# Five pieces of index work moved under the expert loop, and half of the combine's rows gathered before the last expert's are stored

## The chip, the cores and the metric

One NeuronCore of one Trainium2 chip runs the kernel. The metric is the device time of one execution in microseconds. Its engines are TensorE (PE in the profile; PEld is its weight load), VectorE (DVE), ScalarE (ACT), GpSimd (POOL) and SyncE (SP), which only issues transfers here.

## The reference

Two transformer blocks run one after the other on 512 tokens of width 1024, in float32. What the change touches is the end of the second block, a mixture of experts:

```python
g_sel = argmax(g_logits)                     # one group of 4 experts for each token
top_val, top_idx = lax.top_k(e_sel_logits, 2)   # two experts of that group
top_w = softmax(top_val) * g_w
hid = silu(xs @ w_gate[e]) * (xs @ w_up[e])  # 1024 -> 512, for each chosen e
x = x + sum over the two e of top_w * (hid @ w_down[e])   # 512 -> 1024
```

Each token goes to two of 16 experts, so 1024 rows of expert results exist in all, and every token adds two of them, weighted.

## The kernel before, in words

**Everything up to about 1831 us** (the first block, attention and recurrence of the second, the router) is untouched by the change.

**The router** leaves in the tile R (SBUF, one row of small arrays per partition, four tokens to a partition) the choices (R_M), the weights (R_W) and each token's place within its experts (R_P). `rows_of` holds, expert by expert, the 128 tokens that it takes first.

**The expert loop.** Expert e takes up to 128 tokens. GpSimd gathers their rows of `h_rows` from DRAM with an indirect transfer (L2659). PE transposes them (L1182), multiplies by gate and up (`into_hidden`, L1200), transposes the hidden row (`turn_hidden`, L1215) and multiplies by down (`out_of_hidden`, L1220). All products are made in three passes, from an upper and a lower part of each operand, so every weight granule (2 MB) has to be split before use: ACT writes the upper part in two halves (`weights_up`, L1784, instruction L1800), DVE the lower part in two halves (`weights_low`, L2380, instruction L2384). PE waits for each half by `w_low_made`. Raw weights lie in 4 slots, upper halves in 6.

**The order of the work** in the loop is written out by hand on each engine, and each engine runs its own list in order. PE (L1291): gate of e+1, transposes of the hidden row of e, up of e+1, transposes of the tokens of e+2, down of e. DVE (L2412 to L2423): the two lower halves of up e+1, the lower part of hidden row e (`hidden_low`, L2403), the two halves of down e, the product of gate and up of e+1 (`expert_hidden`, L2397), the lower part of the tokens of e+2 (`expert_low`, L2391), and then the two halves of gate e+2. ACT (L1838 to L1851): the two upper halves of up, the Silu of e+1 (L1814), the upper part of hidden row e (L1820), the copy of the result of e-1 out of PSUM (L1826) and its store to `y_rows` in DRAM (L1829), the two upper halves of down e, the tokens' upper part (L1807), the two halves of gate e+2. PE's gate of e+2 starts when its first lower half is made.

**The index work of the combine** stands on DVE behind the loop, L2426 to L2475: 37 small operations, most with a wait on the one before (`chain`). It has two results. `over` (L2447) says how many further tiles of 128 tokens are needed where an expert was chosen by more than 128 tokens; all engines read that count and run a loop of that many trips. `back_rows` (L2475) holds for each token the two rows of `y_rows` that are its results: in columns 0 to 3 the higher row of each of the four tokens, in 4 to 7 the lower.

**The combine.** ACT signals `all_stored` (L1868) once all 16 stores have landed (`y_main`) and further tiles, if any, have too. GpSimd waits for `back_rows` and for `all_stored`, and issues eight gathers of 128 rows of 4 KB (512 KB each, L2676), two for each block of 128 tokens. DVE waits for both rows of a block, adds them to `x_tok` in two operations (L2506), and SP stores the block (L692).

Of the kernel before, what the change touches and what calls it, by code (L numbers as in the profile page):

```python
# [18 lines left out]
U32 = mybir.dt.uint32  # L19
# [173 lines left out]
def program(nc, a, out, known=None, debug=None):  # L193
    n = Counts(known)
    mark, at, now = n.mark, n.at, n.now
    with ExitStack() as ctx:
# [9 lines left out]
        def sem(name):  # L206
            return ctx.enter_context(nc.semaphore(name))
# [29 lines left out]
        back_rows = sb("back_rows", [P, 8], U32)  # L237
        over_i = sb("over_i", [P, 1 + OVER], I32)
# [129 lines left out]
        rows_back = [sem(f"rows_back{i}") for i in range(QT)]  # L368

# [1502 lines left out]
        def _(dve):  # L1872
# [531 lines left out]

            for j in range(4):
                weights_low(j)
# [5 lines left out]
            for e in range(EXPERTS - 1):  # L2412
                j = 2 * granule_no["gate", e + 1]
                weights_low(j + 2)
                weights_low(j + 3)
                hidden_low(e)
                weights_low(j + 4)
                weights_low(j + 5)
                expert_hidden(e + 1)
                if e + 2 < EXPERTS:  # L2420
                    expert_low(e + 2)
                weights_low(j + 6)
                weights_low(j + 7)  # L2423
            hidden_low(EXPERTS - 1)

            chain(stt(out=R[:, R_Q:R_Q + 64], in0=R[:, R_P:R_P + 64], scalar=1.0, in1=R[:, R_M:R_M + 64],  # L2426
                      op0=ALU.add, op1=ALU.mult))
            chain(ts(R[:, R_Q:R_Q + 64], R[:, R_Q:R_Q + 64], -1.0, None, ALU.add))
            places = r(R_Q, QT, 16)

            counts = R[:, R_P + 64:R_P + 80].unsqueeze(1).to_broadcast([P, 3, 16])
            edges = const[:, K_OT:K_OT + 48].rearrange("p (t e) -> p t e", t=3)
            chain(tt(r(R_A, 3, 16), counts, edges, ALU.is_gt))
            flags = R[:, R_A:R_A + 48]
            chain(nc.vector.tensor_tensor_scan(R[:, R_A + 48:R_A + 96], const[:, K_ONES:K_ONES + 48], flags, 0.0,
                                               ALU.mult, ALU.add))
            shape = [P, OVER, 48]
            lst, lst2 = r(R_V, OVER, 48), r(R_V + OVER * 48, OVER, 48)
            chain(tt(lst, R[:, R_A + 48:R_A + 96].unsqueeze(1).to_broadcast(shape),
                     spread(const[:, K_NTH:K_NTH + OVER], 48), ALU.is_equal))  # L2440
            chain(tt(lst, lst, flags.unsqueeze(1).to_broadcast(shape), ALU.mult))
            chain(tt(lst2, lst, const[:, K_OT:K_OT + 48].unsqueeze(1).to_broadcast(shape), ALU.mult))
            chain(nc.vector.tensor_reduce(over_t[:, :], lst2, AX.X, ALU.add))
            chain(tt(lst, lst, const[:, K_OE:K_OE + 48].unsqueeze(1).to_broadcast(shape), ALU.mult))
            chain(nc.vector.tensor_reduce(R[:, R_B + 1:R_B + 1 + OVER], lst, AX.X, ALU.add))
            chain(nc.vector.tensor_copy(R[:, R_B:R_B + 1], R[:, R_A + 95:R_A + 96]))
            made(nc.vector.tensor_copy(over_i[:, :], R[:, R_B:R_B + 1 + OVER]), "over")  # L2447


            first = const[:, K_FIRST:K_FIRST + 16].unsqueeze(1).to_broadcast([P, QT, 16])  # L2450
            chain(tt(r(R_V, QT, 16), r(R_P, QT, 16), first, ALU.add))

            base = R[:, R_A + 48:R_A + 96]
            step = R[:, R_A + 96:R_A + 144]
            chain(ts(base, base, float(P), float((EXPERTS - 1) * P + 1), ALU.mult, ALU.add))
            chain(tt(base, base, const[:, K_OT:K_OT + 48], ALU.subtract))
            chain(tt(step[:, 16:48], base[:, 16:48], base[:, 0:32], ALU.subtract))
            chain(tt(step[:, 0:16], base[:, 0:16], const[:, K_FIRST:K_FIRST + 16], ALU.subtract))
            for t in range(3):
                beyond = r(R_A + 144, QT, 16)  # L2460
                chain(ts(beyond, r(R_P, QT, 16), float(P * (t + 1)), None, ALU.is_ge))
                chain(tt(beyond, beyond, step[:, 16 * t:16 * t + 16].unsqueeze(1).to_broadcast([P, QT, 16]),
                         ALU.mult))
                chain(tt(r(R_V, QT, 16), r(R_V, QT, 16), beyond, ALU.add))
            chain(tt(R[:, R_V:R_V + 64], R[:, R_V:R_V + 64], R[:, R_M:R_M + 64], ALU.mult))
            chain(nc.vector.tensor_reduce(R[:, R_S:R_S + 4], r(R_V, QT, 16), AX.X, ALU.max))
            chain(nc.vector.tensor_reduce(R[:, R_S + 4:R_S + 8], r(R_V, QT, 16), AX.X, ALU.add))
            chain(tt(r(R_A, QT, 16), r(R_V, QT, 16), spread(R[:, R_S:R_S + 4], 16), ALU.is_equal))
            chain(tt(R[:, R_A:R_A + 64], R[:, R_A:R_A + 64], R[:, R_W:R_W + 64], ALU.mult))
            chain(nc.vector.tensor_reduce(R[:, R_WT:R_WT + 4], r(R_A, QT, 16), AX.X, ALU.add))  # L2470
            chain(tt(R[:, R_A:R_A + 64], R[:, R_W:R_W + 64], R[:, R_A:R_A + 64], ALU.subtract))
            chain(nc.vector.tensor_reduce(R[:, R_WT + 4:R_WT + 8], r(R_A, QT, 16), AX.X, ALU.add))
            chain(tt(R[:, R_S + 4:R_S + 8], R[:, R_S + 4:R_S + 8], R[:, R_S:R_S + 4], ALU.subtract))
            chain(ts(R[:, R_S:R_S + 8], R[:, R_S:R_S + 8], -1.0, None, ALU.add))
            made(nc.vector.tensor_copy(back_rows[:, :], R[:, R_S:R_S + 8]), "back_rows")  # L2475
# [26 lines left out]

            for i in range(QT):
                dve.wait_ge(rows_back[i], 32)
                for j in range(2):
                    ins = stt(out=x_tok[:, i, :], in0=returned[:, 2 * i + j, :],  # L2506
                              scalar=R[:, R_WT + 4 * j + i:R_WT + 4 * j + i + 1], in1=x_tok[:, i, :],
                              op0=ALU.mult, op1=ALU.add)
                    if j == 0:

                        ins.then_inc(summed, 1)
                        dve.wait_ge(summed, i + 1)
                ins.then_inc(combined, 1)
# [3 lines left out]
        def _(pool):  # L2517
# [195 lines left out]
```

## Time and profile before

| | |
|---|---|
| three runs | 2173.44 us median (2172.85 to 2177.55) |
| the profiled execution | 2180.36 us |
| its span | 2178.3 us |
| busy: PE, DVE, ACT, POOL | 91%, 59%, 41%, 16% of the span |
| expert loop, about 1831 to 2150 us | per expert some 19.3 us |

The span is what the profiler saw of the engines' work; the execution's own time lies 2.06 us above it. All durations in the text come from the profiled execution.

### The profile page before, as it was taken

Reading aid. Unit: us, or ns where it says so; the run is one execution under the profiler, and the core shown is the slowest. Engines: PE = TensorE matmul, PEld = TensorE weight load, DVE = VectorE, ACT = ScalarE, POOL = GpSimd, SP = SyncE. Lnnn points to the kernel's source line nnn. Section 1 sums busy time; section 2 is a strip of 40 time slices with the busy share of each in tenths; the row PEclk is TensorE's granted clock in tenths of the full one; section 3 lists DMA queues with packets and bytes.
Section 4 is the critical chain, followed back from the end, with each engine's and each line's share of the span. In section 5 each row is a group of like instructions: output and inputs, shape, how many; then the busy total and the mean of one; then the engine's idle time right before and its main releaser. Section 6 shows DMA issues by size and latency. Waiting matters only on the chain.

```text
span 2178.3 us, 27413 instructions
## 1 busy us (share of the span) xinstructions
PE 1983.1 (91%) x11088; PEld 1593.3 (73%) x11088; DVE 1276.1 (59%) x1587; ACT 898.3 (41%) x1476; POOL 351.7 (16%) x259
## 2 busy tenths in 40 slices
PE   5999899999899989999989897888999997999994
PEld 4965678899796667889967695666556876777773
DVE  5449744344444974434448927666665335788886
ACT  3323333333232334333333325543764323777772
POOL 4120122100412012210041104550000001000001
PEclk9999889999799989999989999999999996999997
DMA  4202110223220111022212220012124233999994
GB/s 141 79 24 63 39 40 20 78 80 96 66 78 25 50 52 40 22 76 90 95 64 73 77 68 30 20 40 77 60 76 164 97 135 115 373 386 383 381 373 189
DMA packets 159873, 241.58 MB, mean 111 GB/s; under 512 B 8754, under 2 KB 106195, under 8 KB 159747
## 3 DMA queue, kind: packets, MB, share of 16 engines
q1 hardware_dynamic: 152370, 213.01, 29.0%
q0 software_dynamic: 4464, 16.25, 2.0%
q10 hardware_dynamic: 2912, 10.55, 1.2%
q8 instruction: 90, 1.47, 0.3%
q14 instruction: 37, 0.30, 0.0%
HBM read 223.55 MB, written 16.25 MB: 110 GB/s over the span
## 4 chain that ended last, share of the span: by engine, by line
PE 73%; DVE 20%; issue 2%; ACT 2%; DMA 1%; POOL 0%; ACTq 0%; POOLq 0%; DVEq 0%
PE acc L756 28%; PE acc L983 15%; PE acc L1196 8%; DVE work L1943 5%; PE acc L968 4%; PE acc L735 3%; PE acc L913 3%; PE acc L1048 2%; PE acc L890 2%; DVE ring_split L2384 2%; DVE v L2128 1%; PE acc L1106 1%; DVE rt L2198 1%; PE acc L901 1%; DVE ring L1959 1%
## 5 line engine op out<-in xcount | busy, mean ns | idle before, releaser
L756 PE MATMUL acc<-h_split,ring_split 128*128 128x264 f32 x1088 | 312.9, 288 | 0.0
L756 PE MATMUL acc<-h_split,v_split 128*128 128x264 f32 (+1 forms) x736 | 212.5, 289 | 9.8 <-DVE ring_split L1948 8.5
L756 PE MATMUL acc<-ring_split,v_split 128*128 128x264 f32 (+1 forms) x736 | 209.8, 285 | 0.0
L756 PEld LDWEIGHTS acc<-h_split,ring_split 128*128 128x128 f32 x1088 | 209.4, 192 | 0.0
L1948 DVE TENSOR_TENSOR ring_split<-ring,v_split 128x1024 fp32r<-128x1024 f32 (+1 forms) x78 | 92.3, 1185 | 177.6 <-ACT v_split L1355 177.6
L756 PEld LDWEIGHTS acc<-h_split,v_split 128*128 128x128 f32 (+1 forms) x736 | 138.9, 189 | 13.3 <-issue 9.8
L983 PE MATMUL acc<-h_split,ring_split 128*128 128x512 f32 x368 | 145.4, 395 | 0.0
L1943 DVE RECIPROCAL work<-work 96x528 f32<-96x528 f32 (+1 forms) x38 | 130.9, 3445 | 24.2 <-ACT work L1385 23.8
L756 PEld LDWEIGHTS acc<-ring_split,v_split 128*128 128x128 f32 (+1 forms) x736 | 139.0, 189 | 0.1
L735 PE MATMUL acc<-latent,ring 128*96 128x264 f32 (+1 forms) x512 | 119.9, 390 | 0.0
L1355 ACT ACTIVATE v_split<-ring 128x1024 fp32r<-128x1024 f32 x80 | 77.5, 971 | 84.6 <-PE acc L756 80.0
L756 PE MATMUL acc<-h_split,krope_split 128*128 128x264 f32 x320 | 95.6, 299 | 16.2 <-DVE work L2017 13.2
L735 PEld LDWEIGHTS acc<-latent,ring 128*96 128x96 f32 (+1 forms) x512 | 77.5, 156 | 42.8 <-issue 9.4
L2128 DVE RECIPROCAL v<-v 128x512 f32<-128x512 f32 x26 | 87.1, 3351 | 24.7 <-ACT v L1564 24.7
L2067 DVE TENSOR_TENSOR acc<-acc,const 128x128 f32<-128x128 f32 (+1 forms) x80 | 21.7, 272 | 132.5 <-PE acc L890 132.2
L756 PE MATMUL acc<-ring_split,krope_split 128*128 128x264 f32 x320 | 92.2, 288 | 0.0
L2551 POOL TENSOR_TENSOR ring_split<-ring,krope_split 128x1024 fp32r<-128x1024 f32 x20 | 47.3, 2363 | 265.1 <-ACT krope_split L1355 265.1
L2538 POOL TENSOR_TENSOR latent<-latent 128x528 f32<-128x528 f32 x21 | 32.0, 1525 | 322.3 <-ACT latent L1350 321.8
L1196 PE MATMUL acc<-qk_split,krope_split 128*128 128x512 f32 x240 | 75.8, 397 | 8.6 <-DVE ring_split L2384 6.2
L2659 POOL DMA_INDIRECT latent<-h_rows,rows_of x16 | 18.3, 1145 | 396.7 <-PE acc L1182 229.4
L983 PEld LDWEIGHTS acc<-h_split,ring_split 128*128 128x128 f32 x368 | 69.7, 189 | 16.2
L913 PE MATMUL acc<-latent,v 128*64 128x128 f32 (+2 forms) x480 | 79.1, 289 | 0.0
(485 smaller groups left out, 5407.6 us busy)
## 6 DMA issues: line engine op xcount, KB each, us to landing
ring<-in_w_in SPq DMA_DIRECT2D x64, 1024.0 KB, 5.2
ring<-in_w_expert_gate SPq DMA_DIRECT2D x13, 2048.0 KB, 10.4
ring<-in_w_expert_up SPq DMA_DIRECT2D x12, 2048.0 KB, 11.3
ring<-in_w_expert_down SPq DMA_DIRECT2D x11, 2048.0 KB, 11.7
ring<-in_w_out SPq DMA_DIRECT2D x12, 1024.0 KB, 5.3
hres<-in_w_expert_down SPq DMA_DIRECT2D x5, 2048.0 KB, 11.2
hres<-in_w_expert_up SPq DMA_DIRECT2D x4, 2048.0 KB, 11.2
y_rows<-gate ACTq DMA_DIRECT2D x16, 512.0 KB, 7.1
```

Of the source, the lines that this page charges most:

```text
L735: ins = nc.tensor.matmul(dst[at_row:at_row + rows_, half, 0:HALF], w, rhs(k)[:, half * HALF:(half + 1) * HALF], start=(k == 0), stop=(k == ...
L756: ins = nc.tensor.matmul(dst[0:rows_, half, 0:HALF], w[:, k, :], x[:, c], start=(k == 0 and i == 0), stop=(k == last and i == 2), skip_gro ...
L890: ins = nc.tensor.matmul(dst[0:nt, c0:c1], qT[0:QK, hd, t0:t0 + nt], kT[0:QK, hd, c0:c1], start=True, stop=True)
L913: ins = nc.tensor.matmul(dst[r:r + VD, 0, 0:nt], v[0:nk, j, hd * VD:(hd + 1) * VD], probsT[s % 2][0:nk, j, 0:nt], start=(j == 0), stop=(j ...
L968: ins = nc.tensor.matmul(dst[:, 0, :], w, rhs(k), start=(k == 0), stop=(k == len(lhs) - 1))
L983: ins = nc.tensor.matmul(dst[:, 0, :], w[:, k, :], x, start=(k == 0 and i == 0), stop=(k == DC - 1 and i == 2), skip_group_check=True)
L1196: ins = nc.tensor.matmul(dst, x, w, start=start and i == 0, stop=stop and i == 2, skip_group_check=True)
L1355: nc.scalar.activation(dst, src, ACT.Copy).then_inc(act_made, 1)
L1943: chain(nc.vector.reciprocal(work[0:rows_, tile, :], work[0:rows_, tile, :]))
L1948: made(nc.vector.tensor_tensor(dst, src, up.bitcast(F32), ALU.subtract), label)
L2128: chain(nc.vector.reciprocal(tmp[tile], tmp[tile]))
L2551: nc.gpsimd.tensor_tensor(dst, src, up.bitcast(F32), ALU.subtract).then_inc(pool_made, 1)
```

## The change

The 37 operations are the same but for two more, and are cut into five functions. They are called on DVE in the trips e = 3, 5, 7, 9 and 11 of the expert loop, between `expert_low(e + 2)` and the two lower halves of gate e+2. The last of them makes a second list, `early_rows`: the lower row of each token, limited to the rows of the first 15 experts. GpSimd gathers these four lists once the results of the first 15 experts have landed, before it reads `over`. Once all is stored it gathers only the four lists of higher rows. If there are further tiles, it gathers the lower rows again after them. DVE adds the four early rows first, then the four late ones. The early rows go to places 0 to 3 of `returned`, the late ones to places 4 to 7, which overlap the buffers of upper halves.

```diff
@@ DVE, in the expert loop
                 if e + 2 < EXPERTS:
                     expert_low(e + 2)
+                if e == 3:
+                    places_of_rows()
+                elif e == 5:
+                    over_rows()
+                elif e == 7:
+                    main_rows()
+                elif e == 9:
+                    later_rows()
+                elif e == 11:
+                    rows_of_tokens()
                 weights_low(j + 6)
                 weights_low(j + 7)
@@ DVE, the end of rows_of_tokens (the rest of the five is L2426 to L2475 in the same order)
+                chain(ts(R[:, R_S + 8:R_S + 12], R[:, R_S + 4:R_S + 8], float((EXPERTS - 1) * P - 1), None, ALU.min))
+                nc.vector.tensor_copy(early_rows[:, :], R[:, R_S + 8:R_S + 12])
                 made(nc.vector.tensor_copy(back_rows[:, :], R[:, R_S:R_S + 8]), "back_rows")
@@ DVE, the combine (inside "if tiles > 0", behind its loop: wait for rows_early[i] >= 32)
-            for i in range(QT):
-                dve.wait_ge(rows_back[i], 32)
-                for j in range(2):
...
+            for i in range(QT):
+                dve.wait_ge(rows_early[i], 16)
+                add_row(i, i, R_WT + QT + i).then_inc(summed, 1)
+            for i in range(QT):
+                dve.wait_ge(rows_back[i], 16)
+                dve.wait_ge(summed, i + 1)
+                add_row(i, QT + i, R_WT + i).then_inc(combined, 1)
@@ GpSimd
+            pool.wait_ge(dve_made, at(dve_made, "back_rows"))
+            pool.wait_ge(y_main, 16 * (EXPERTS - 1))
+            for i in range(QT):
+                nc.gpsimd.indirect_dma_start(returned[:, i, :], None, y_rows[0:(EXPERTS - 1) * P, :],
+                                             bass.IndirectOffsetOnAxis(early_rows[:, i:i + 1], 0))\
+                    .then_inc(rows_early[i], 16)
             pool.wait_ge(dve_made, at(dve_made, "over"))
             tiles = pool.value_load(over_i[0:1, 0:1], min_val=0, max_val=OVER)
             with pool.If(tiles > 0):
...
+                pool.wait_ge(all_stored, 1)
+                for i in range(QT):
+                    pool.wait_ge(rows_early[i], 16)
+                    nc.gpsimd.indirect_dma_start(returned[:, i, :], None, y_rows,
+                                                 bass.IndirectOffsetOnAxis(back_rows[:, QT + i:QT + i + 1], 0))\
+                        .then_inc(rows_early[i], 16)
-            pool.wait_ge(dve_made, at(dve_made, "back_rows"))
             pool.wait_ge(all_stored, 1)
             for i in range(QT):
-                for j in range(2):
-                    nc.gpsimd.indirect_dma_start(returned[:, 2 * i + j, :], None, y_rows,
-                                                 bass.IndirectOffsetOnAxis(back_rows[:, 4 * j + i:4 * j + i + 1], 0))\
-                        .then_inc(rows_back[i], 16)
+                nc.gpsimd.indirect_dma_start(returned[:, QT + i, :], None, y_rows,
+                                             bass.IndirectOffsetOnAxis(back_rows[:, i:i + 1], 0))\
+                    .then_inc(rows_back[i], 16)
```

## Rows read from the trace of the kernel before

**Rows 1.** The page: its first line, and section 4, the chain by engine.

```profile
span 2178.3 us, 27413 instructions
...
PE 73%; DVE 20%; issue 2%; ACT 2%; DMA 1%; POOL 0%; ACTq 0%; POOLq 0%; DVEq 0%
```

**Rows 2.** Waits of PE, 1880 to 2145: total us, times, longest.

```profile
PE acc L1196 <- DVE ring_split L2384: 10.2, 20, 1.4
PE acc L1196 <- DVE hres_split L2384: 3.6, 7, 0.6
PE acc L1196 <- ACT gate L1826: 1.8, 1, 1.8
```

**Rows 3.** Windows, expert loop; after the busy times: PEclk, DMA share, GB/s.

```profile
1960.00:2145.00 185.00, 173.21 (x793) 138.44 (x792) 152.27 (x91) 133.52 (x96) 6.70 (x7) 1.00 0.95 351
```

**Rows 4.** Chain, 1960 to 2002: start, us, what.

```profile
1969.10 5.81 PE acc L1196 x24
...
1982.08 2.32 DVE ring_split L2384
...
1986.13 2.21 DVE hres_split L2384
...
1988.47 5.70 PE acc L1196 x24
```

**Rows 5.** ACT timeline, 1910 to 1990: start, us, operation, [idle before it <-releaser].

```profile
1975.44 0.60 ACT L1814 ACTIVATE v<-acc 128x512 f32<-128x512 f32 x1 [4.79 <-PE acc L1217]
...
1977.92 3.72 ACT L1800 ACTIVATE qk_split<-ring 128x2048 fp32r<-128x2048 f32 x2 [0.47 <-ACT gate L1826]
```

**Rows 6.** DVE timeline, 1910 to 1990.

```profile
1976.56 0.69 DVE L2403 TENSOR_TENSOR krope_split<-acc,krope_split 128x512 fp32r<-128x512 f32 x1 [1.01 <-ACT krope_split L1820]
1979.87 4.53 DVE L2384 TENSOR_TENSOR ring_split<-ring,qk_split 128x2048 fp32r<-128x2048 f32 x2 [2.62 <-ACT qk_split L1800]
```

**Rows 7.** DVE timeline, 2110 to 2179: first operation of each piece, and the last.

```profile
2144.25 0.22 DVE L2426 SCALAR_TENSOR_TENSOR o<-o 128x64 f32<-128x64 f32 x1
...
2146.35 0.51 DVE L2442 TENSOR_TENSOR o<-o,const 128x336 f32<-128x336 f32 x1
...
2148.78 0.22 DVE L2451 TENSOR_TENSOR o<-o,const 128x64 f32<-128x64 f32 x1
...
2149.93 0.20 DVE L2461 TENSOR_SCALAR o<-o 128x64 f32<-128x64 f32 x1
...
2152.18 0.23 DVE L2465 TENSOR_TENSOR o<-o 128x64 f32<-128x64 f32 x1
...
2154.63 0.17 DVE L2475 CAST back_rows<-o 128x8 uint32<-128x8 f32 x1
```

**Rows 8.** Chain, 2140 to 2179.

```profile
2151.47 2.64 DMA y_rows<-gate
...
2155.95 0.94 POOL qk L2676
```

**Rows 9.** ACT timeline, 2140 to 2179.

```profile
2144.45 0.34 ACTq L1829 DMA_DIRECT2D y_rows<-gate  x1
```

**Rows 10.** Line 2676, the eight gathers: durations, first and last start, landing.

```profile
L2676 POOL DMA_INDIRECT qk<-y_rows,back_rows x8: 936/938/1310, 2156.0 to 2165.0; - x8
...
DMA to landing us min/median/max: 4.1/6.1/7.7
```

**Rows 11.** DVE timeline, 2110 to 2179: sums that waited for rows.

```profile
2166.09 5.12 DVE L2506 SCALAR_TENSOR_TENSOR work<-qk,o,work 128x1024 f32<-128x1024 f32 x4 [0.87 <-DMA qk<-y_rows,back_rows]
2172.72 2.61 DVE L2506 SCALAR_TENSOR_TENSOR work<-qk,o,work 128x1024 f32<-128x1024 f32 x2 [1.50 <-DMA qk<-y_rows,back_rows]
```

**Rows 12.** Line 1829, the sixteen stores of expert results: landing.

```profile
DMA to landing us min/median/max: 2.6/7.1/7.9
```

**Rows 13.** DMA issues, 2165.2 to 2165.6: size, us to landing.

```profile
out<-work SPq DMA_DIRECT2D x1, 512.0 KB, 6.8
```

**Rows 14.** DMA issues, 2168 to 2170.

```profile
out<-work SPq DMA_DIRECT2D x1, 512.0 KB, 4.9
```

More of the change, by code:

```diff
@@ L237, in program @@
         back_rows = sb("back_rows", [P, 8], U32)
+        early_rows = sb("early_rows", [P, QT], U32)
         over_i = sb("over_i", [P, 1 + OVER], I32)
@@ L368, in program @@
         rows_back = [sem(f"rows_back{i}") for i in range(QT)]
+        rows_early = [sem(f"rows_early{i}") for i in range(QT)]
         held = sem("held")
@@ L2403, in hidden_low, with places_of_rows @@
                 evacuated(tt(ht_low, acc[:, 3, 0, :], ht_up.bitcast(F32), ALU.subtract), ("ht", e))
+            places = r(R_Q, QT, 16)
+            shape = [P, OVER, 48]
+            lst, lst2 = r(R_V, OVER, 48), r(R_V + OVER * 48, OVER, 48)
+            flags = R[:, R_A:R_A + 48]
+            base = R[:, R_A + 48:R_A + 96]
+            step = R[:, R_A + 96:R_A + 144]
+            def places_of_rows():
+                chain(stt(out=R[:, R_Q:R_Q + 64], in0=R[:, R_P:R_P + 64], scalar=1.0, in1=R[:, R_M:R_M + 64],
+                          op0=ALU.add, op1=ALU.mult))
+                chain(ts(R[:, R_Q:R_Q + 64], R[:, R_Q:R_Q + 64], -1.0, None, ALU.add))
+                counts = R[:, R_P + 64:R_P + 80].unsqueeze(1).to_broadcast([P, 3, 16])
+                edges = const[:, K_OT:K_OT + 48].rearrange("p (t e) -> p t e", t=3)
+                chain(tt(r(R_A, 3, 16), counts, edges, ALU.is_gt))
+                chain(nc.vector.tensor_tensor_scan(R[:, R_A + 48:R_A + 96], const[:, K_ONES:K_ONES + 48], flags, 0.0,
+                                                   ALU.mult, ALU.add))
+                chain(tt(lst, R[:, R_A + 48:R_A + 96].unsqueeze(1).to_broadcast(shape),
+                         spread(const[:, K_NTH:K_NTH + OVER], 48), ALU.is_equal))
+                chain(tt(lst, lst, flags.unsqueeze(1).to_broadcast(shape), ALU.mult))
@@ new lines, in over_rows @@
+            def over_rows():
+                chain(tt(lst2, lst, const[:, K_OT:K_OT + 48].unsqueeze(1).to_broadcast(shape), ALU.mult))
+                chain(nc.vector.tensor_reduce(over_t[:, :], lst2, AX.X, ALU.add))
+                chain(tt(lst, lst, const[:, K_OE:K_OE + 48].unsqueeze(1).to_broadcast(shape), ALU.mult))
+                chain(nc.vector.tensor_reduce(R[:, R_B + 1:R_B + 1 + OVER], lst, AX.X, ALU.add))
+                chain(nc.vector.tensor_copy(R[:, R_B:R_B + 1], R[:, R_A + 95:R_A + 96]))
+                made(nc.vector.tensor_copy(over_i[:, :], R[:, R_B:R_B + 1 + OVER]), "over")
@@ new lines, in main_rows @@
+            def main_rows():
+                first = const[:, K_FIRST:K_FIRST + 16].unsqueeze(1).to_broadcast([P, QT, 16])
+                chain(tt(r(R_V, QT, 16), r(R_P, QT, 16), first, ALU.add))
+                chain(ts(base, base, float(P), float((EXPERTS - 1) * P + 1), ALU.mult, ALU.add))
+                chain(tt(base, base, const[:, K_OT:K_OT + 48], ALU.subtract))
+                chain(tt(step[:, 16:48], base[:, 16:48], base[:, 0:32], ALU.subtract))
+                chain(tt(step[:, 0:16], base[:, 0:16], const[:, K_FIRST:K_FIRST + 16], ALU.subtract))
@@ L2424, in _ @@
             hidden_low(EXPERTS - 1)
[L2426 to L2447, printed above, removed]
@@ L2450, in _ @@
[L2450 to L2471, printed above, removed]
@@ L2472, in _ @@
[L2472 to L2475, printed above, removed]
             def hidden(tag):
@@ L2501, in _, with add_row @@
                     n.leave()
-            for i in range(QT):
-                dve.wait_ge(rows_back[i], 32)
-                for j in range(2):
[L2506 to L2513, printed above, removed]
+                for i in range(QT):
+                    dve.wait_ge(rows_early[i], 32)
+            def add_row(i, row, weight_):
+                return stt(out=x_tok[:, i, :], in0=returned[:, row, :], scalar=R[:, weight_:weight_ + 1],
+                           in1=x_tok[:, i, :], op0=ALU.mult, op1=ALU.add)
+            for i in range(QT):
+                dve.wait_ge(rows_early[i], 16)
[4 more added lines that the diff above has]
+                add_row(i, QT + i, R_WT + i).then_inc(combined, 1)
         @block.gpsimd
```

19 lines of the change are left out of this document (added).

## The prediction

> **What bounds the kernel now.** I read the page first: PE is 73% of the chain that ended last, DVE 20% [rows 1]. That share is an average, so the next question was who ends PE's waits in the stretch where the new work is put. Over the expert loop PE waits 15.6 us, and 13.8 of them, in 27 waits, end with a lower half made by DVE (L2384) [rows 2]; the TensorE clock there is 1.00, its 2.4 GHz level, and DMA is 95% busy [rows 3].
>
> The chain of waits then shows where in an expert this happens. One period is 19.37 us, from the start of one gate product to the next (1969.10 to 1988.47) [rows 4]. It closes as a ring with no slack in it. The gate product ends at 1974.91 and four transposes follow; ACT has sat idle 4.79 us for them and starts at 1975.44 [rows 5]. It works through Silu, hidden row, result copy and store issue, and begins the upper halves of down at 1977.92. DVE has been idle for the first of these halves for 2.62 us and starts at 1979.87 [rows 6]. From there it never stops: two lower halves, the product (L2397), the tokens' lower part (L2391), and from 1986.13 the first lower half of the next gate, on which PE starts at 1988.47 [rows 4]. The new pieces go between L2391 and that half: on the ring, in front of the instruction that PE waits for.
>
> At the end the order is another. The index work runs from 2144.25 to 2154.80 [rows 7] beside PE's last down product, ACT's last copy and the last store, which is issued at 2151.47 and lands 2.64 us later; after some handing over GpSimd starts its gathers at 2155.95 [rows 8]. back_rows is ready 1.15 us before that. So the index work costs nothing today, and taking it away from there gains nothing. The real gain has to come from what lies behind 2155.95: eight gathers, eight sums, stores, 22.35 us up to the span's end at 2178.3.
>
> **The change, step by step. The five pieces in the loop.** Their costs are differences of starts in the trace of today [rows 7]: 2.10 us (2144.25 to 2146.35), 2.43, 1.15, 2.25, and for the last piece 2.45 to the start of L2475, 0.17 for it, and two new operations of the same small kind, which I price at 0.20 and 0.17 after their neighbours: 2.99. Together 10.92 us. Each piece stands in one period on the ring, so PE's gate starts that much later, ACT's Silu after it as well, and every later period with it. Nothing gives it back: PE already waits in front of that product (0.4 us of its wait is there now), and DVE's two idle stretches, 1.01 and 2.62 us [rows 6], end with ACT operations that themselves follow the delayed gate. The bounds are 10.9 (all exposed) and 0 (all absorbed in those 3.6 us per expert, more than any one piece takes); I take **+10.9**, because the ring accounts for the whole period.
>
> The waits that the pieces add (`chain`) are waits of DVE on itself and are inside the differences. Queued behind them on DVE are the gate halves, which is the cost just counted. ACT, SP and GpSimd get no new wait in the loop. GpSimd's gathers of tokens come once per expert and shift with PE.
>
> **The late gathers.** Now four follow `all_stored` in place of eight. A lone gather lands 4.1 us after its issue, and issues are 1.29 us apart ((2165.0 - 2156.0)/7) [rows 10]. So the fourth can't land before 3 x 1.29 + 4.1 = 8.0 us after the first issue. With four more behind it it has landed 10.1 us after (2166.09, where DVE waits for its second block) [rows 11]. I take 10.0: the other four gathers are gone, but the stores of blocks 0 to 2 now begin while gathers are still running, and block 0's store took 6.8 us and block 1's 4.9 us among gathers [rows 13, 14], so the engines stay full. Then one sum of 1.28 us (5.12/4) instead of two [rows 11], and the last store with its end, 2.97 us today (2178.3 less 2172.72 + 2.61); it will have one or two others ahead of it, so 3.1, at most 4.9 as with block 1. Sum: 10.0 + 1.3 + 3.1 = 14.4 us in place of 22.35, **-8.0** (ends: 8.0 + 1.3 + 3.0 = 12.3 gives -10.0; 10.1 + 1.3 + 4.9 = 16.3 gives -6.1).
>
> **The early gathers.** They wait for back_rows, long ready, and for 15 stores. The fifteenth is issued at 2144.45 [rows 9] and lands by about 2147.1 at the 2.6 us that an undisturbed store takes [rows 12]. With 0.8 us for GpSimd to get going, as ahead of 2155.95, they are issued from about 2147.9 to 2151.8 and land between 2152.0 and 2158.0 (+4.1 and +10.1 as above). Their four sums, 5.1 us of DVE, run until about 2159 while DVE has nothing else: hidden, unless the late rows arrive before then. GpSimd's reading of `over` stands behind them and before `all_stored`: hidden too.
>
> But the last expert's store is issued at 2151.47, in the middle of them. It took 2.64 us with the engines to itself [rows 8]. What a 512 KB store takes beside gathers is seen twice: 6.8 us with four or five outstanding, 4.9 with two and another store [rows 13, 14]; here three are outstanding at its issue. Beside the weight loads the stores took 7.1 in the median, 7.9 at most [rows 12]. I take 5.8, the mean of the two that stand beside gathers: **+3.2**, with 0 and +5.3 as ends. Everything late waits for this store, so it counts in full.
>
> A page of the Trainium skill bears on this from both sides. "DMA: Bandwidth & Descriptors", section "Queues, rings and completion order", says that the write which counts a transfer as done lands only after every earlier write of that DMA engine, over all its queues. By that rule the store can't be counted before the gathers' parts already written ahead of it, which speaks against this change and for the upper half of my range. The same section says that a DMA engine takes turns between the queues that have work, packet by packet, which speaks for a mild delay, the second rival below. The two stores among gathers agree with a delay, and do not say which of the two rules makes it.
>
> **Sum.** +10.9 - 8.0 + 3.2 = +6.1 us on the profiled execution's span. That execution took 2180.36, above the median of the three runs, 2173.44; the difference of some microseconds lies outside what the change touches, so I add the change to the median: 2179.5 us, 0.28% slower. A measurement of this kernel can tell about 0.2% from no change, 4.3 us.
>
> **Rivals.**
>
> 1. *Absorbed (faster).* DVE's idle 3.6 us per expert takes up each piece, because ACT's part of the ring turns out to be held by something else (a weight transfer, with DMA 95% busy [rows 3]) that does not move with the gate product. Then +0 - 8.0 + 3.2 = -4.8: 2168.6 us. It decides for faster once over 9.5 of the 10.9 us are absorbed, and for a tie from about 2. For it: the idle time exists and is longer than the longest piece. Against it: ACT's 4.79 us end with PE, not with a transfer [rows 5], and PE's waits end with exactly the instruction that is pushed back. 12%.
>
> 2. *The store is hardly delayed (a tie).* The queues take turns and the store pays no more than its own data once over: at most 1.3 us, half of its 2.64. Then 10.9 - 8.0 + 0 to 1.3 = +2.9 to +4.2: 2176.3 to 2177.6. For it: the first early gather lands about when the store is issued, and much of the rest is through by 2156. Against: 6.8 and 4.9 [rows 13, 14]. 20%.
>
> 3. *The overlap does not happen (slower still).* The early gathers move nothing ahead; the store stands behind all of them, until 2158.0 + 1.3 = 2159.3 in place of 2154.1, +5.2. Then 10.9 - 8.0 + 5.2 = +8.1: 2181.5. For it: the skill's rule of ordered counting, and stores of 7.1 us beside weight loads. Against: by the end only the fourth gather is still running. 10%.
>
> **How the numbers follow.** The forecast has 58%. Of its own spread a small part falls below +4.3 us. Slower by over 0.2%: 58 + 10, less 4 for that part, 64%. Within 0.2%: 20 + 4, 24%. Faster: 12%. The range goes from the best of both tail terms, 10.9 - 10.0 + 0 = +0.9 (2174.3), to the worst, 10.9 - 6.1 + 5.3 = +10.1 (2183.6). That leaves out rival 1 and little besides; I open the lower end slightly, to 2174.0.
>
> **What would show it right or wrong.** In the profile after: periods with a piece (e = 3, 5, 7, 9, 11) longer than their neighbours by 2.1, 2.4, 1.2, 2.3 and 3.0 us, with PE's wait before the gate product grown from 0.4 by the same, and the others unchanged at 19.3. If those waits grow and the period does not, the ring was not one. The last store takes 5 to 7 us in place of 2.64; if it takes under 4, rival 2 holds, and at 7.8 rival 3. From the first late gather to the span's end: about 14.4 us. The operations' own durations should not change. The granted clock must stay 1.00 through the lengthened waits, up to 3.4 us each; the loop today has one wait of 1.8 [rows 2] at that clock [rows 3], and a fall to the 1.2 GHz level would make PE the slowest part and put the time above my range.

## The result, and the profile after

The changed kernel took 2186.21 us in the median of six runs (2181.06 to 2190.51), the kernel before 2173.14 (2169.40 to 2177.55): a ratio of 1.0054, with a 95% interval of 1.0037 to 1.0070, so 8 to 15 us slower. Forecast were +6.1 us and 2179.5; the direction held, the time lies outside the range.

The profiled execution of the changed kernel took 2190.51 us, its span is 2188.3. The page of the profile has the same shape as [rows 1]:

```profile
span 2188.3 us, 27422 instructions
...
PE 74%; DVE 20%; issue 2%; ACT 2%; DMA 1%; POOL 0%; ACTq 0%; POOLq 0%; DVEq 0%
```

A difference of spans (10.0 us) mixes two things. The part before the expert loop, which the change does not touch, varied by several microseconds between executions: ACT's first Silu of the loop, counted from the table load on its line, starts at 1850.35 in the profile before and at 1844.43 here, 5.9 us earlier. The granted clock varies there, too (0.95 of full speed over the first 400 us before, 0.97 here). I therefore measure every kernel from that Silu on. From it to the span's end it is 327.95 us before and 343.87 after, **+15.9 us**, in four terms:

| | before | after | difference | forecast |
|---|---|---|---|---|
| loop: first Silu to the last lower part of a hidden row | 293.30 | 310.11 | +16.8 | +10.9 |
| last down product: from there to the last store's issue | 7.82 | 9.42 | +1.6 | 0 |
| last store's issue to the first late gather | 4.48 | 8.98 | +4.5 | +3.2 |
| first late gather to the end of the span | 22.35 | 15.36 | -7.0 | -8.0 |

**The loop.** The timeline of ACT has each expert's Silu, which follows the gate product. These are six of them (start, duration, operation, idle time before and who ended it):

```profile
1934.60 0.60 ACT L1816 ACTIVATE v<-acc 128x512 f32<-128x512 f32 x1 [8.45 <-PE acc L1219]
...
1953.87 0.60 ACT L1816 ACTIVATE v<-acc 128x512 f32<-128x512 f32 x1 [4.65 <-PE acc L1219]
...
1977.10 0.60 ACT L1816 ACTIVATE v<-acc 128x512 f32<-128x512 f32 x1 [8.69 <-PE acc L1219]
...
1996.35 0.60 ACT L1816 ACTIVATE v<-acc 128x512 f32<-128x512 f32 x1 [4.62 <-PE acc L1219]
...
2016.85 0.60 ACT L1816 ACTIVATE v<-acc 128x512 f32<-128x512 f32 x1 [5.95 <-PE acc L1219]
...
2036.12 0.60 ACT L1816 ACTIVATE v<-acc 128x512 f32<-128x512 f32 x1 [4.65 <-PE acc L1219]
```

A period is 19.3 us, as in the kernel before, when it has no piece (1934.60 to 1953.87). Those with one are 23.23 us (the second piece, 1953.87 to 1977.10) and 20.50 us (the third, 1996.35 to 2016.85). The third piece is 1.15 us long and costs 1.16. The second is 2.43 us and costs 3.9. The first, fourth and fifth cost 3.65, 3.66 and 4.35 for 2.10, 2.25 and 2.99. So each of the four longer pieces costs its own length and 1.4 to 1.6 us more (periods of the kernel before: 19.34 us in the same trips).

DVE's timeline shows that the second piece itself has the length of [rows 7]: it starts with the second line here, the weight half behind it starts 2.42 us later with the last, and nothing in it is stretched:

```profile
1963.30 1.22 DVE L2393 TENSOR_TENSOR v_split<-acc,v_split 128x1024 fp32r<-128x1024 f32 x1
1964.43 0.50 DVE L2430 TENSOR_TENSOR o<-o,const 128x336 f32<-128x336 f32 x1
...
1966.77 0.17 DVE L2435 CAST over_i<-o 128x8 int32<-128x8 f32 x1
1966.85 2.28 DVE L2386 TENSOR_TENSOR ring_split<-ring,zp_split 128x2048 fp32r<-128x2048 f32 x1
```

What is stretched is PE's work behind it. PE's timeline:

```profile
1966.07 0.39 PE L1198 MATMUL acc<-hres_split,krope_split 128*128 128x512 f32 x1
1969.28 1.19 PE L1198 MATMUL acc<-zp_split,v_split 128*128 128x512 f32 x2 [2.82 <-DVE ring_split L2386]
...
1970.69 1.06 PE L1198 MATMUL acc<-zp_split,v_split 128*128 128x512 f32 x2
...
1972.92 0.62 PE L1198 MATMUL acc<-zp_split,v_split 128*128 128x512 f32 x2
```

And the windows of the same stretch (length, busy time of PE, PEld, DVE, ACT and POOL, then the granted clock, DMA share, GB/s):

```profile
1966.00:1969.00 3.00, 0.46 (x3) 0.03 (x1) 2.90 (x5) 2.41 (x2) 0.00 (x0) 1.00 1.02 414
1969.00:1970.00 1.00, 0.72 (x2) 0.66 (x3) 1.00 (x2) 0.00 (x0) 0.00 (x0) 0.55 0.97 367
1970.00:1971.00 1.00, 1.00 (x4) 0.81 (x3) 1.00 (x1) 0.00 (x0) 0.00 (x0) 0.50 1.04 397
...
1972.00:1973.00 1.00, 1.00 (x5) 0.82 (x4) 1.00 (x1) 0.00 (x0) 0.00 (x0) 0.75 1.05 389
1973.00:1974.00 1.00, 1.00 (x6) 0.83 (x5) 1.00 (x2) 0.00 (x0) 0.00 (x0) 1.00 1.06 389
```

PE's wait before the gate product has grown from 0.40 to 2.82 us. When PE resumes, the granted clock is 0.50, the 1.2 GHz level, until about 1972.5, and two matmuls take 1.06 us where they take 0.62 at 1.00. That is the other 1.5 us (3.9 less 2.43). The first, fourth and fifth piece have such a fall too, after waits of 2.51, 2.64 and 3.20 us, each some 3 us long; the third, after a wait of 1.55, has none. The waits of PE in total over the loop (here 1880 to 2163), against [rows 2], have grown by the pieces' own length (10.2 to 20.9) and don't contain it, since a slow product is no wait:

```profile
PE acc L1198 <- DVE ring_split L2386: 20.9, 20, 3.2
PE acc L1198 <- DVE hres_split L2386: 3.6, 7, 0.6
PE acc L1198 <- ACT gate L1828: 1.8, 1, 1.8
```

**The last down product.** It fell to the low level as well, from about 2156.9 to 2160.2 (clock 0.50 in the windows 2157 to 2160), though nothing in the change lengthens the waits before it: 1.37 us for the last lower half and 1.80 us for ACT's copy, 1.39 and 1.80 before. ACT then waited 7.62 us for it where it was 6.00.

**The last store and the gathers.** ACT's timeline has the last copy and store:

```profile
2162.91 1.02 ACT L1828 ACTIVATE gate<-acc 128x1024 f32<-128x1024 f32 x1 [7.62 <-PE acc L1198]
2163.96 0.34 ACTq L1831 DMA_DIRECT2D y_rows<-gate  x1
```

GpSimd's timeline, first and last of the early and of the late gathers:

```profile
2158.73 0.93 POOL L2692 DMA_INDIRECT qk<-y_rows,early_rows  x1 [72.80 <-DMA y_rows<-gate]
...
2162.45 0.94 POOL L2692 DMA_INDIRECT qk<-y_rows,early_rows  x1 [0.31 <-issue]
2172.94 0.94 POOL L2714 DMA_INDIRECT qk<-y_rows,back_rows  x1 [9.55 <-ACTq L1870]
...
2176.67 0.93 POOL L2714 DMA_INDIRECT qk<-y_rows,back_rows  x1 [0.30 <-issue]
```

DVE's timeline, first and last early sum, first and last late one:

```profile
2162.98 1.28 DVE L2532 SCALAR_TENSOR_TENSOR work<-qk,o,work 128x1024 f32<-128x1024 f32 x1 [7.75 <-DMA qk<-y_rows,early_rows]
...
2170.13 1.28 DVE L2532 SCALAR_TENSOR_TENSOR work<-qk,o,work 128x1024 f32<-128x1024 f32 x1 [1.16 <-DMA qk<-y_rows,early_rows]
2177.14 1.28 DVE L2532 SCALAR_TENSOR_TENSOR work<-qk,o,work 128x1024 f32<-128x1024 f32 x1 [5.72 <-DMA qk<-y_rows,back_rows]
...
2182.92 1.28 DVE L2532 SCALAR_TENSOR_TENSOR work<-qk,o,work 128x1024 f32<-128x1024 f32 x1 [0.77 <-DMA qk<-y_rows,back_rows]
```

The early gathers are issued from 2158.73 to 2162.45 and the fourth lands at 2170.13, 11.4 us after the first issue. The last store, issued at 2163.96 with three of them outstanding, lands 7.7 us later by the list of DMA issues:

```profile
y_rows<-gate ACTq DMA_DIRECT2D x1, 512.0 KB, 7.7
```

The late gathers therefore begin 8.98 us after its issue, not 4.48 [rows 8]. From there on four gathers and four sums take 15.36 us in place of 22.35.

### The profile page after: what moved, and what is told of

Same layout as the page of the kernel before. It is cut to its first block, busy times and chain, and to the rows that moved or that the text cites. A ratio compares the mean times of both kernels' runs of the same rounds, so it can differ in the third digit from the quotient of the medians.

```text
span 2188.3 us, 27422 instructions
## 1 busy us (share of the span) xinstructions
PE 1986.9 (91%) x11088; PEld 1597.1 (73%) x11088; DVE 1276.5 (58%) x1589; ACT 896.7 (41%) x1476; POOL 351.2 (16%) x259
## 4 chain that ended last, share of the span: by engine, by line
PE 74%; DVE 20%; issue 2%; ACT 2%; DMA 1%; POOL 0%; ACTq 0%; POOLq 0%; DVEq 0%
PE acc L758 28%; PE acc L985 15%; PE acc L1198 9%; DVE work L1945 5%; PE acc L970 4%; PE acc L737 3%; PE acc L915 3%; PE acc L1050 2%; DVE ring_split L2386 2%; PE acc L892 2%; PE acc L1108 1%; DVE rt L2200 1%; PE acc L903 1%; PE acc L840 1%; DVE ring L1961 1%
## 5 line engine op out<-in xcount | busy, mean ns | idle before, releaser
L758 PE MATMUL acc<-h_split,krope_split 128*128 128x264 f32 x320 | 95.9, 300 | 16.5 <-DVE work L2019 13.1
```

The source lines that it names most:

```text
L758: ins = nc.tensor.matmul(dst[0:rows_, half, 0:HALF], w[:, k, :], x[:, c], start=(k == 0 and i == 0), stop=(k == last and i == 2), skip_gro ...
```

## The experiments

Two theories stood at the start. **A**: the pieces stand on the ring and are exposed in full, and where one makes PE wait 2.5 us or more before the gate product, the clock's fall adds 1.4 to 1.5 us. **Proportional**: each microsecond of a piece costs about 1.5 on the ring, whatever the cause (16.8/10.9). Beside them: the extra comes from the combine's transfers (B), or from the small operations disturbing other engines wherever they stand (C). For the end of the kernel: **S**, the last store pays for the early gathers beside it.

**e1_lists_only** keeps the pieces in the loop and puts the combine back:

```diff
-            pool.wait_ge(y_main, 16 * (EXPERTS - 1))
-            for i in range(QT):
-                nc.gpsimd.indirect_dma_start(returned[:, i, :], None, y_rows[0:(EXPERTS - 1) * P, :],
-                                             bass.IndirectOffsetOnAxis(early_rows[:, i:i + 1], 0))\
-                    .then_inc(rows_early[i], 16)
...
             pool.wait_ge(all_stored, 1)
             for i in range(QT):
-                nc.gpsimd.indirect_dma_start(returned[:, QT + i, :], None, y_rows,
-                                             bass.IndirectOffsetOnAxis(back_rows[:, i:i + 1], 0))\
-                    .then_inc(rows_back[i], 16)
+                for j in range(2):
+                    nc.gpsimd.indirect_dma_start(returned[:, 2 * i + j, :], None, y_rows,
+                                                 bass.IndirectOffsetOnAxis(back_rows[:, 4 * j + i:4 * j + i + 1], 0))\
+                        .then_inc(rows_back[i], 16)
```

> The five pieces in the expert loop as in the change, the combine as before (eight gathers behind the last store). All is measured on the trace from the start of the first Silu of the loop: 327.95 us to the span's end in the kernel before, 343.87 in the changed one. Theory A (ring and clock): the pieces cost their own 10.9 us on the ring, and four of them (all but the 1.15 us one) some 1.4 to 1.5 us each again, because PE's wait of 2.5 us or more before the gate product is followed by products at the 1.2 GHz level. So the loop, first to last hidden-row lower part, is 16.8 us longer than before (as in the changed kernel), and the end, from the last store's issue on, is as before: 26.8 us. Together +16.8, about 2190 us against 2173. Theory B (the extra 5.9 us of the loop come from the new order of the transfers of the combine): the loop is only 10.9 us longer.

Measured: 2193.32 us in the median, ratio 1.0084 (1.0062 to 1.0106). From the first Silu on 345.43 us, +17.5: the loop +16.7, the last product as before, the last store's issue to the end 27.6 (26.8 before). The granted clock falls in the same four periods as in the changed kernel. The loop's extra is there without the new combine: B falls.

**e2_idle_place** calls the same five pieces four calls earlier in the same trips, in front of the lower halves of down, where DVE sat idle for ACT:

```diff
                 hidden_low(e)
+                if e == 3:
+                    places_of_rows()
...
+                elif e == 11:
+                    rows_of_tokens()
                 weights_low(j + 4)
                 weights_low(j + 5)
                 expert_hidden(e + 1)
                 if e + 2 < EXPERTS:
                     expert_low(e + 2)
-                if e == 3:
-                    places_of_rows()
...
-                elif e == 11:
-                    rows_of_tokens()
                 weights_low(j + 6)
```

> The change with the five pieces called one place earlier in the trip, between the hidden row's lower part and the two lower halves of down, where DVE sits idle 2.6 us for ACT. Theory A (ring and clock): pieces up to 2.6 us cost nothing there and the last, 2.99 us, costs 0.4; no wait of PE grows by more than that and the clock stays at 2.4 GHz. The loop is 0.4 us longer than before, the end 2.5 us shorter than before (last store +4.5, late gathers and sums -7.0), in all -2 us: about 2171, unless the clock falls in the last down product as in the changed kernel (+1.6). Theory C (the small operations and their waits disturb wherever they stand, by slowing ACT or the transfers): the loop stays 10 us or more longer than before.

Measured: 2170.61 us, ratio 0.9980 (0.9965 to 0.9995), a little faster than the kernel before. From the first Silu on 326.15 us, -1.8: the loop +0.36, the end from the last store's issue 24.7 (-2.2, expected -2.5): the last store took 6.9 us and the late gathers began 8.2 us after its issue. The waits of PE are nearly those of [rows 2] again:

```profile
PE acc L1198 <- DVE ring_split L2386: 10.4, 20, 1.4
PE acc L1198 <- DVE hres_split L2386: 3.7, 7, 0.7
```

And the clock in the window from 1880 to 2142 is 1.00:

```profile
1880.00:2142.00 262.00, 246.11 (x1126) 196.73 (x1125) 222.97 (x162) 188.38 (x135) 10.89 (x11) 1.00 0.97 359
```

The same 39 operations in the same trips, four calls earlier in DVE's list, cost 0.36 us and not 16.8. C falls.

**e3_twelve_pieces** leaves the place and cuts finer. The five functions become one generator of the same operations in the same order, which stops after each of twelve pieces:

```diff
-                if e == 3:
-                    places_of_rows()
...
-                elif e == 11:
-                    rows_of_tokens()
+                if 2 <= e <= 13:
+                    next(rows_pieces)
                 weights_low(j + 6)
```

> The change with the same operations in the same place of the trip, but cut into twelve pieces of 0.3 to 1.1 us in the trips 2 to 13. Theory A: all 10.9 us are still exposed, but no wait of PE before the gate product goes over 1.6 us, so the granted clock stays 1.00: the loop is 10.9 us longer than before, 5.9 less than with the change, and no period has products at 0.50. Rival (proportional cost: each us of a piece costs 1.5 us on the ring, whatever its length): 16.8 us longer, as in the changed kernel.

Measured: 2181.86 us, ratio 1.0031 (1.0008 to 1.0053). The loop is +10.9 us, the whole from the first Silu 336.76, +8.8. The granted clock in its window from 1880 to 2142 is 1.00:

```profile
1880.00:2142.00 262.00, 238.08 (x1086) 190.19 (x1086) 214.16 (x157) 180.40 (x129) 9.56 (x10) 1.00 0.95 348
```

In the same window of the changed kernel it is 0.97:

```profile
1880.00:2142.00 262.00, 239.44 (x1067) 191.57 (x1067) 210.91 (x155) 176.23 (x128) 10.01 (x11) 0.97 0.96 354
```

PE's waits in e3 are 1.6 us at most (against 3.2 in the changed kernel), and their sum is as large:

```profile
PE acc L1198 <- DVE ring_split L2386: 18.9, 20, 1.6
PE acc L1198 <- DVE hres_split L2386: 5.1, 6, 1.4
```

The same work in the same place cost 5.9 us less once no single wait was long. The proportional reading falls; A stands on both of its numbers.

**e4_one_piece** does the opposite:

```diff
-                if e == 3:
-                    places_of_rows()
...
-                elif e == 11:
-                    rows_of_tokens()
+                if e == 11:
+                    places_of_rows()
+                    over_rows()
+                    main_rows()
+                    later_rows()
+                    rows_of_tokens()
```

> The change with all five pieces in one trip (e = 11), 10.9 us at once. Theory A: one wait of PE of 11.3 us and one fall of the clock instead of four; the products behind it run at 0.50 a little longer than behind a short wait. The loop is 10.9 plus 1.5 to 3.5 us longer than before, 12.4 to 14.4. Rival (proportional): 16.8 us. If a fall cost the same whatever came before, 12.4.

Measured: 2184.92 us, ratio 1.0049 (1.0036 to 1.0063). The loop is +13.5 us: 10.9 and one fall worth 2.6. PE waits 11.13 us once, and its matmuls take 1.06 us a pair from 2089.4 until about 2095, longer than behind the 2.82 us wait. Its timeline:

```profile
2077.92 0.39 PE L1198 MATMUL acc<-ring_split,krope_split 128*128 128x512 f32 x1
2089.44 1.19 PE L1198 MATMUL acc<-zp_split,v_split 128*128 128x512 f32 x2 [11.13 <-DVE ring_split L2386]
...
2093.42 1.06 PE L1198 MATMUL acc<-zp_split,v_split 128*128 128x512 f32 x2
...
2095.61 0.62 PE L1198 MATMUL acc<-upad_split,v_split 128*128 128x512 f32 x2
```

So a fall is no fixed sum: 1.4 to 1.6 us after waits of 2.5 to 3.2, 2.6 after 11.

The other four start from e2_idle_place, where the loop is clean, and look at the end.

**e6_no_early** takes the early gathers and their sums away (each token's lower row is left out of the result):

```diff
-            pool.wait_ge(y_main, 16 * (EXPERTS - 1))
-            for i in range(QT):
-                nc.gpsimd.indirect_dma_start(returned[:, i, :], None, y_rows[0:(EXPERTS - 1) * P, :],
-                                             bass.IndirectOffsetOnAxis(early_rows[:, i:i + 1], 0))\
-                    .then_inc(rows_early[i], 16)
...
-            for i in range(QT):
-                dve.wait_ge(rows_early[i], 16)
-                add_row(i, i, R_WT + QT + i).then_inc(summed, 1)
...
-                dve.wait_ge(summed, i + 1)
```

> e2_idle_place without the four early gathers and their four sums (each token's lower row is left out of the result). It measures the late part by itself. Theory S: the last store takes 2.6 us, the late gathers begin 4.5 us after its issue, and from their first issue to the end it is 14.4 to 15.4 us (15.4 in the changed kernel, 16.4 in e2, 22.35 before). Rival R (the late part is 16.4 us because four gathers and four output stores alone take that): 16.4 here too. In e2 the late gathers began while an early row was still on its way, so below 16.4 is expected.

Measured (one execution, 2170.32 us): the last store takes 2.6 us, by the list of DMA issues in e2 and here:

```profile
y_rows<-gate ACTq DMA_DIRECT2D x1, 512.0 KB, 6.9
...
y_rows<-gate ACTq DMA_DIRECT2D x1, 512.0 KB, 2.6
```

The late gathers begin 3.94 us after its issue (4.5 expected), and it is 15.7 us from there to the end (14.4 to 15.4 expected; 15.4 in the changed kernel, 16.4 in e2). The store's delay is the early gathers' doing. The late part costs 15.7 with no early row beside it, so my 14.4 was too little and not spoiled by the early rows.

**e7_lists_idle_only** is e1 with the pieces in the idle place:

```diff
                 hidden_low(e)
+                if e == 3:
+                    places_of_rows()
...
+                elif e == 11:
+                    rows_of_tokens()
                 weights_low(j + 4)
...
                     expert_low(e + 2)
-                if e == 3:
-                    places_of_rows()
...
-                elif e == 11:
-                    rows_of_tokens()
                 weights_low(j + 6)
```

> e1_lists_only (the combine as before, eight gathers behind the last store) with the pieces in the place where DVE is idle. Theory A: the loop is 0.4 us longer than before and the end as before, 26.8 us; +0.4, no difference that can be measured. Together with e2 it gives the worth of the early gathers by themselves: -2.2 us. Theory C (the index work costs wherever it stands in the loop) was 10 us or more and would show here too.

Measured: 2176.51 us, ratio 1.0016 (1.0003 to 1.0028); from the first Silu on 329.0 us, +1.1: the loop +0.4, the end 27.45 us where it was 26.83 (eight gathers took 23.0 us in place of 22.35, as they took 23.1 in e1). The index work by itself is not a gain in either place, as it was hidden before. The early gathers are worth 329.0 - 326.15 = 2.9 us in the profiles (2.2 expected). The medians of e7 and e2 lie 5.9 us apart, but they come from different sets of runs.

**e8_two_early** gathers only blocks 0 and 1 early:

```diff
-            for i in range(QT):
+            for i in range(2):
                 nc.gpsimd.indirect_dma_start(returned[:, i, :], None, y_rows[0:(EXPERTS - 1) * P, :],
...
             for i in range(QT):
+                if i >= 2:
+                    nc.gpsimd.indirect_dma_start(returned[:, i, :], None, y_rows,
+                                                 bass.IndirectOffsetOnAxis(back_rows[:, QT + i:QT + i + 1], 0))\
+                        .then_inc(rows_early[i], 16)
                 nc.gpsimd.indirect_dma_start(returned[:, QT + i, :], None, y_rows,
```

(DVE adds the lower rows of blocks 2 and 3 inside its late loop, each before that block's higher row).

> e2_idle_place with only the lower rows of blocks 0 and 1 gathered early, those of blocks 2 and 3 behind the last store. Theory S (traffic is only exchanged): the last store is delayed by the data of two gathers less, so it takes some 4.5 us in place of 6.9, and the late part, now six gathers, grows from 16.4 to about 19 us. From the last store's issue to the end 4.5 + 1.8 + 19 = 25 us, within 1 us of e2's 24.7. If the delay of the store came at once with any gather (whatever their number), it would take 6.9 and the end be 27 or more.

Measured: 2171.16 us, ratio 0.9994 (0.9984 to 1.0005). In its profile the last down product fell to the low clock again (+1.7 us), which put off the last store's issue so far that the first gather had landed and the second landed 1.1 us later: the store took 2.6 us, the late gathers began 3.94 us after its issue, undelayed, and took 20.0 us to the end (19 expected). From the store's issue 24.0 us, e2 24.7. The exchange of traffic comes out about even, as S says, but the delay of the store by two gathers was not seen, so this run doesn't test it.

**e5_swapped_experts** came out of S: if the early gathers cost because they meet the last store, they should end before it. That needs rows whose results are complete earlier. A token's two experts are of one group, so with experts 3 and 14 exchanged in the order of the work the last two worked on are of different groups, and every token's first row lies among the first 14 results:

```diff
+ORDER = [14 if e == 3 else 3 if e == 14 else e for e in range(EXPERTS)]
-    t[:, K_FIRST:K_FIRST + 16] = P * np.arange(16) + 1
+    t[:, K_FIRST:K_FIRST + 16] = P * np.array(ORDER) + 1
...
-            pool.wait_ge(y_main, 16 * (EXPERTS - 1))
+            pool.wait_ge(y_main, 16 * (EXPERTS - 2))
```

(the weights' loads and `rows_of` take `ORDER[e]`, the limit of `early_rows` is 14 experts).

> e2_idle_place with experts 3 and 14 changed about in the order of the work, so that the last two experts worked on are of different groups and each token's first row lies among the first 14 results; the early gathers wait for 14 stores in place of 15. Theory S (the last store pays for the early gathers): they land by the time the last store is issued, so it takes 2.6 us again in place of 6.9, GpSimd's late gathers begin 4.5 us after its issue in place of 8.2, and from its issue to the span's end it is 19 to 20 us (24.7 in e2, 26.8 in the kernel before). From the first Silu of the loop on about 321 us, 7 less than before (327.95), about 2168 in all. The store of expert 15's forerunner now has the gathers beside it and takes 6 to 7 us in place of 2.6; that costs up to 1 us if the last copy has to wait for it. Rival (the store is slow for another reason, or the late part grows by what the store gains): no better than e2, 24.7 us from the last store's issue on.

Measured: 2166.68 us, ratio 0.9966 (0.9954 to 0.9979). GpSimd's timeline, first and last early gather and the first late one:

```profile
2131.54 2.08 POOL L2693 DMA_INDIRECT qk<-y_rows,early_rows  x1 [55.87 <-DMA y_rows<-gate]
...
2138.92 1.90 POOL L2693 DMA_INDIRECT qk<-y_rows,early_rows  x1 [0.30 <-issue]
2153.37 0.94 POOL L2715 DMA_INDIRECT qk<-y_rows,back_rows  x1 [12.55 <-ACTq L1871]
```

ACT's timeline, last copy and store:

```profile
2148.38 1.02 ACT L1829 ACTIVATE gate<-acc 128x1024 f32<-128x1024 f32 x1 [7.69 <-PE acc L1199]
2149.43 0.34 ACTq L1832 DMA_DIRECT2D y_rows<-gate  x1
```

The early rows are all in by 2145.6, the store is issued at 2149.43 and takes 2.6 us, and the late gathers begin 3.94 us after it. The store before it, issued at 2140.72 beside the last early gathers, took 5.3 us (6 to 7 expected), and the last copy did not wait for it. To the end it is 19.6 us from the store's issue (26.8 before, 24.7 in e2), as expected. From the first Silu on 322.84 us, -5.1 against the kernel before where 7 were expected; the last down product fell to the low clock here as well and took 1.7 us of it (ACT waits 7.69 us for it). This kernel has the lowest median of all; its interval and e2's (0.9965 to 0.9995) overlap, and the two were measured in different sets of runs, so the medians do not separate them. The traces do: 19.6 us against 24.7 from the last store's issue.

## Why the prediction was wrong

**The place and the ring: right.** Every piece was exposed by its own length, 10.9 us in all, as e3 shows without anything else, and the idle 2.6 us next to it would have taken them (e2: 0.36).

**The step that failed: "Together 10.92 us ... Each piece stands in one period on the ring, so PE's gate starts that much later".** The term was mis-sized: it was 16.8. I priced the delay of PE's start and held its products at their old duration. The clock stood in the text only as a condition at the very end ("must stay 1.00 through the lengthened waits"), with no rival, no price and no share of the range, though the longest wait that the trace before had shown at full clock was 1.8 us and by my own prices four of my pieces made waits of 2.5 to 3.4. With 5.9 us for it the forecast would have been +12.0. My rival for "slower still" was a different mechanism, a store behind all gathers. The condition said that a fall "would make PE the slowest part and put the time above my range". The second half came true; the first did not, each fall lasted some 3 us and cost 1.4 to 1.6.

**The last store: right in kind, small in size.** It took 7.7 us where I took 5.8, and in e2 6.9. The handing over behind it was shorter by half a microsecond, so the term was +4.5 in the changed kernel and +3.7 in e2 against +3.2. (In e5, e6 and e8 the late gathers begin 3.94 us after the issue of a store that takes 2.6; in the kernel before, e1 and e7 it is 4.47 to 4.48. No run isolates why.) Rival 2, a store hardly delayed, falls in both.

Rival 3, the store behind all gathers, is not refuted. By my own sign, 7.8 for it against 5 to 7, the changed kernel's 7.7 stands on its side: all four gathers had been issued, the fourth landed at 2170.1, and the store landed 1.5 us later. In e2, e3 and e4 the fourth gather was issued 0.1 to 0.2 us after the store; there the store took 6.9, 6.9 and 6.5 us, landing behind the third gather and before the fourth. That fits a store that stands behind what was issued before it, and does not exclude that all of them merely shared the engines. Of the two rules of the Trainium skill's page "DMA: Bandwidth & Descriptors", section "Queues, rings and completion order", I had read the one of taking turns too kindly: my reading gave at most 3.9 us for the store, and 6.5 to 7.7 were measured. The one of ordered counting agrees with a long delay and with these orders of landing, but no run here isolates it. What e6 shows is that the early gathers cause the delay, by whichever rule.

**The late part: right in kind, large by 1.** -7.0, where I said -8.0: 15.4 to 16.5 us in place of 14.4. The fourth row did land 10.0 us after the first issue (2182.92 - 2172.94), as I took it. It was the last output store, beside those of other blocks, that took 3.7 us and so ended 4.1 us after the last sum, in place of 3.1. In e2, where this part took 16.4 us, GpSimd also needed 1.96 and 1.77 us for two of the four issues in place of 0.94, and the fourth row landed 12.1 us after the first issue.

**The last down product: not foreseen.** A fall there came in the changed kernel, e5 and e8 (+1.6, +1.7 and +1.7) and not in the profiles of the kernel before, e1, e2, e3, e4, e6 and e7. The waits ahead of it were 1.37 and 1.80 us in the changed kernel and 1.39 and 1.90 in e5 and e8, against 1.37 to 1.39 and 1.80 in all the others; e1 has the changed kernel's pair and no fall. Each kernel has one profile, so why it comes, and whether it comes in every execution of a kernel, stays open; e2, e3 and e4 have the changed kernel's code at the end and show none. Without it the profile's difference is +14.3, inside the measured interval of +8 to +15 us, while +15.9 lies just above it. The untouched part before the loop moved by up to 13 us between the profiles (the first Silu between 1839.3 and 1852.6), more than most differences studied here, which is why the terms are read from the traces and the medians only bound their sum.

**A slip in rival 1.** By my own sum of +6.1 and limit of 4.3 us, the change would be faster only once over 10.4 of the 10.9 us were absorbed, not 9.5.

## What to carry to other kernels

Before putting work into a loop for free, look for the engine's idle stretch and who ends it, and place the piece in front of that wait, not in front of the instruction that another engine waits for: here two places in one list, four calls apart, differed by 16.4 us. Price a lengthened wait of PE with the products behind it as well, and if work must stand in such a place, cut it fine (twelve pieces cost 10.9 us, five 16.8). A transfer moved ahead of a critical one can delay it, here from 2.6 us to between 6.5 and 7.7; ask whether the data can be complete early enough for the transfer to be over by then.

## What the runs showed of the hardware

A PE wait of 1.6 us or less before the gate product was followed by products at the full clock in all periods of e3; waits of 2.5 to 3.2 us were followed by about 3 us at the 1.2 GHz level in the changed kernel and e1; and one of 11.1 us by almost 6 us of it in e4. That is not a rule for every product: before the last down product, waits of 1.37 and 1.80 us, or 1.39 and 1.90, came ahead of a fall in three profiles, and waits of 1.37 to 1.39 and 1.80 ahead of none in the other seven. GpSimd's issue of a gather took 0.94 us in most cases, but 1.9 to 2.5 us for all four early ones of e5, which run beside the end of the loop, and 1.7 to 2.0 us for two late ones of e2 and one each of e3 and e4; no experiment here isolates why. In all ten profiles each issue of a combine gather that took over 1.1 us began while a DVE operation was running, and each that began with DVE idle took 0.93 or 0.94 us. The reverse does not hold (0.94 us at 2170.93 in e4 and 1.04 at 2182.32 in e1 began beside DVE too), so this is no explanation yet.
